# Last expert's rows of the others, constants issued from ScalarE, and output halves stored before the overflow loop

## What is computed

```python
for i in range(DEPTH):                       # DEPTH = 2
    h = rms_norm(x, ln_mix[i])
    y = dilated_attention(h, ...) if i == 0 else rwkv7_bidirectional(h, ...)
    x = x + y
    h = rms_norm(x, ln_ffn[i])
    x = x + (swiglu(h, f_w13, f_w2) if i == 0 else moe_swiglu(h, router, w13, w2))

def moe_swiglu(h, router, w13, w2):          # 8 experts, the best 2 of each token
    top_val, top_idx = lax.top_k((t @ router), 2)
    gate = jax.nn.softmax(top_val, axis=-1)
    for e in range(8):
        out = out + combine[:, e:e + 1] * swiglu(t, w13[e], w2[e])
```

## Time and profile before

| | |
|---|---|
| time, median of 3 runs | 1946.71 us (1943.17 to 1948.93) |
| time of the profiled execution | 1941.92 us |
| its span | 1940.0 us |
| PE busy | 1851.5 us (95%) |
| DVE, ACT, POOL busy | 761.2, 286.0, 198.0 us |
| read from HBM | 460.04 MB |

### The profile page before, as it was taken

How to read it: one execution, slowest core, us unless ns; L and a number is a source line. 1 busy time by engine, 2 the same in 40 slices (tenths; PEclk the granted TensorE clock), 3 DMA queues, 4 the chain that set the end, 5 groups by cost and what they waited for, 6 DMA issues and landing times.

```text
span 1940.0 us, 35245 instructions
## 1 busy us (share of the span) xinstructions
PE 1851.5 (95%) x15348; PEld 1123.1 (58%) x15348; DVE 761.2 (39%) x2119; ACT 286.0 (15%) x611; POOL 198.0 (10%) x318
## 2 busy tenths in 40 slices
PE   7998998999998999889879999999999999999997
PEld 3445445677763558788745555555555555555453
DVE  3114113100007255866335535344353534445333
ACT  2113113000000225434210000000000000000000
POOL 1110110100001233642200000000000000000000
PEclk9999999999998999999989999999999999999998
DMA  9442351635542101100267999999999999999992
GB/s 362 170 137 80 132 172 44 195 131 173 148 173 87 38 9 23 29 21 7 93 261 281 414 404 407 406 392 417 399 415 402 405 409 395 415 404 406 416 371 99
DMA packets 137631, 472.49 MB, mean 244 GB/s; under 512 B 30104, under 2 KB 59056, under 8 KB 94464
## 3 DMA queue, kind: packets, MB, share of 16 engines
q1 hardware_dynamic: 134592, 460.05, 61.6%
q0 software_dynamic: 2080, 7.37, 1.2%
q10 hardware_dynamic: 800, 2.76, 0.4%
HBM read 460.04 MB, written 10.10 MB: 242 GB/s over the span
## 4 chain that ended last, share of the span: by engine, by line
PE 87%; DVE 6%; ACT 2%; DMA 2%; issue 1%; SPq 0%; POOL 0%; DVEq 0%; POOLq 0%
PE ps L1275 19%; PE ps L679 13%; PE ps L801 13%; PE ps L1251 10%; PE ps L1283 10%; PE ps L739 8%; PE ps L1258 5%; PE ps L752 3%; PE ps L855 2%; PE ps L768 1%; DMA arena<-yd,arena 1%; PE ps L1199 1%; DVE arena L1883 1%; PE ps L687 1%; PE ps L1206 1%
## 5 line engine op out<-in xcount | busy, mean ns | idle before, releaser
L1275 PE MATMUL ps<-arena 128*64 128x256 f32 x3584 | 397.1, 379 | 0.7 <-DVE arena L2096 0.7
L679 PE MATMUL ps<-arena 128*128 128x128 f32 (+11 forms) x2114 | 334.2, 332 | 33.4 <-DVE arena L1870 9.1
L1275 PEld LDWEIGHTS ps<-arena 128*64 128x64 f32 x3584 | 255.9, 137 | 151.2 <-issue 29.0
L679 PEld LDWEIGHTS ps<-arena 128*128 128x128 f32 (+4 forms) x2114 | 248.2, 187 | 111.1 <-issue 56.5
L801 PE MATMUL ps<-arena 128*128 128x512 f32 x576 | 251.6, 592 | 2.0 <-DMA arena<-wqkv 2.0
L2146 DVE TENSOR_TENSOR arena<-arena,ps 64x256 f32<-64x256 f32 x168 | 71.3, 426 | 395.4 <-ACT arena L1583 395.2
L1283 PE MATMUL ps<-arena 128*32 128x256 f32 x3584 | 205.7, 381 | 0.5 <-issue 0.5
L1251 PE MATMUL ps<-arena 128*64 128x512 f32 x896 | 203.3, 598 | 0.0
L801 PEld LDWEIGHTS ps<-arena 128*128 128x128 f32 x576 | 107.4, 190 | 127.7 <-issue 125.3
L1583 ACT ACTIVATE arena<-ps 64x256 f32<-64x256 f32 x168 | 63.2, 376 | 751.2 <-PE ps L1275 550.3
L1283 PEld LDWEIGHTS ps<-arena 128*32 128x32 f32 x3584 | 111.6, 110 | 89.1 <-issue 22.4
(11 more groups left out here) (249 smaller groups left out, 1222.5 us busy)
## 6 DMA issues: line engine op xcount, KB each, us to landing
arena<-mw SPq DMA_DIRECT2D x336, 1024.0 KB, 11.8
arena<-wqkv SPq DMA_DIRECT2D x36, 1024.0 KB, 8.6
arena<-fw SPq DMA_DIRECT2D x32, 1024.0 KB, 6.7
arena<-wrkv SPq DMA_DIRECT2D x12, 1024.0 KB, 6.4
arena<-awo SPq DMA_DIRECT2D x4, 1024.0 KB, 6.2
arena<-bwo SPq DMA_DIRECT2D x4, 1024.0 KB, 9.9
xg<-arena POOLq DMA_DIRECT2D x8, 384.0 KB, 9.4
arena<-xg SPq DMA_DIRECT2D x7, 384.0 KB, 15.7
```

Of the source, the lines that this page charges most:

```text
L679: last = mm(o, a, b, start=(n == 0), stop=(n == len(pairs) - 1))
L1275: last = mm(ps[r, g % 4, 0:256], picked[:, b, k, 0:64], w[:, k, a * 256:(a + 1) * 256], start=(k == 0), stop=(k == KB - 1))
```

## The change

It has four parts.

1. The five small loads leave SP's queue and are issued by ACT, as its first instructions, `vec` ahead of `const`. SP goes from x straight to `wqkv`.
2. In the last expert, `add_rows` is no longer called once after j = 2 (the first pair). `add_rows(0)` adds the first row of each token after j = 8, and `add_rows(1)` the second after j = 11.
3. `scatter` writes its four products to four PSUM banks (4, 7, 0, 1), and PE's waits on `back_sb` are gone.
4. SP stores each half of x as soon as `add_back` is done with it, and only then reads `many` and goes through its overflow loop. Stores inside that loop would repeat the output if a body were entered. `experts_done` is gone, and at the end SP waits for both stores.

```diff
--- before.py
+++ after.py
@@ -498,11 +497,6 @@
 
             for t in range(T):
                 sp.dma_start(x[:, t, :], x_in[t * P:(t + 1) * P, :]).then_inc(in_x[t], 16)
-            sp.dma_start(const[:, 0:C_TRI], const_in[:, 0:C_TRI]).then_inc(in_const, 16)
-            sp.dma_start(vec, vec_in).then_inc(in_vec, 16)
-            sp.dma_start(pos_i, pos_in).then_inc(in_small, 16)
-            sp.dma_start(qkc, qk_cols).then_inc(in_small, 16)
-            sp.dma_start(qkr, qk_rows.partition_broadcast(P)).then_inc(in_small, 16)
             for u in range(U_QKV):
                 if u == 6:
                     sp.dma_start(const[:, C_TRI:C_ALL], const_in[:, C_TRI:C_ALL]).then_inc(in_mask, 16)
@@ -651,12 +645,16 @@
                 expert_unit(item, EXPERTS // 2 - 1)
                 next_rows(item, EXPERTS // 2 - 1)
 
+            for t in range(T):
+                sp.wait_ge(back_sb, 2 * t + 2)
+                sp.dma_start(out[t * P:(t + 1) * P, :], x[:, t, :]).then_inc(out_done, 16)
             sp.wait_ge(over_ok, 1)
             many = sp.value_load(over_i[0:1, 0:1], min_val=0, max_val=OVER)
             with sp.Fori(0, OVER) as j:
                 with sp.If(j < many):
                     e = sp.value_load(over_i[0:1, bass.ds(j + (OVER + 1), 1)], min_val=0, max_val=EXPERTS - 1)
                     sp.wait_ge(down_ps, j * (GE // 2) + EXPERTS * GE // 2)
+                    sp.wait_ge(out_done, j * 32 + 32)
                     freed = [(up_ps, 3 * (n // 2) + 3) if kind == "up" else (down_ps, n + 1) for kind, n, _ in over_plan]
                     for kind, n, u in over_plan:
                         if u >= R:
@@ -664,9 +662,10 @@
                             per = UPS if s is up_ps else GE // 2
                             sp.wait_ge(s, j * per + (EXPERTS * per + c))
                         tiled_unit(u, (mw13 if kind == "up" else mw2)[bass.ds(e, 1), n])
-            sp.wait_ge(experts_done, 1)
-            sp.dma_start(out.rearrange("(t p) n -> p t n", p=P), x).then_inc(out_done, 16)
-            sp.wait_ge(out_done, 16)
+                    for t in range(T):
+                        sp.wait_ge(back_sb, j * 4 + (2 * t + 6))
+                        sp.dma_start(out[t * P:(t + 1) * P, :], x[:, t, :]).then_inc(out_done, 16)
+            sp.wait_ge(out_done, 32)
 
 
         @block.tensor
@@ -1239,9 +1238,7 @@
                 pe.wait_ge(pickT_sb, back)
                 for k in range(4):
                     t, h = k // 2, k % 2
-                    if k >= 2:
-                        pe.wait_ge(back_sb, back * 4 + (k - 5))
-                    run(ps[:, (4, 7)[k % 2], :], [(pickT[0:width, b, t, :], yb[0:width, h * 512:(h + 1) * 512])]).then_inc(back_ps, 1)
+                    run(ps[:, (4, 7, 0, 1)[k], :], [(pickT[0:width, b, t, :], yb[0:width, h * 512:(h + 1) * 512])]).then_inc(back_ps, 1)
 
             def expert(n, c, b, plan, landed, before_last=None):
 
@@ -1330,6 +1327,12 @@
 
         @block.scalar
         def _(act):
+            act.dma_start(vec, vec_in).then_inc(in_vec, 16)
+            act.dma_start(const[:, 0:C_TRI], const_in[:, 0:C_TRI]).then_inc(in_const, 16)
+            act.dma_start(pos_i, pos_in).then_inc(in_small, 16)
+            act.dma_start(qkc, qk_cols).then_inc(in_small, 16)
+            act.dma_start(qkr, qk_rows.partition_broadcast(P)).then_inc(in_small, 16)
+
             steps = Steps(act, act_step)
 
             def rms_squares(n, junk, added=None):
@@ -2115,7 +2118,7 @@
                     t, h = n // 2, n % 2
                     cols = slice(h * 512, (h + 1) * 512)
                     dve.wait_ge(back_ps, c * 4 + (n - 3))
-                    dve.scalar_tensor_tensor(x[:, t, cols], ps[:, (4, 7)[n % 2], :], weight(t), x[:, t, cols], ALU.mult, ALU.add).then_inc(back_sb, 1)
+                    dve.scalar_tensor_tensor(x[:, t, cols], ps[:, (4, 7, 0, 1)[n], :], weight(t), x[:, t, cols], ALU.mult, ALU.add).then_inc(back_sb, 1)
 
             def first_turned(pair):
 
@@ -2137,7 +2140,7 @@
                         last = dve.transpose(o[:, a, :, 64:CAP], src[:, :, j, :])
                 return last
 
-            def expert(n, stored, at_second=None, next_b=None):
+            def expert(n, stored, add_rows=None, next_b=None):
 
                 for j in range(UPS):
                     p = j // 3
@@ -2152,8 +2155,8 @@
                     if j % 3 == 2:
                         dve.wait_ge(hide_sb, n * UPS + (j + 1))
                         last_turned(p).then_inc(hidT_sb, 1)
-                    if j == 2 and at_second:
-                        at_second()
+                    if j in (8, 11) and add_rows is not None:
+                        add_rows((j - 8) // 3)
                     if j in (11, 14) and next_b is not None:
                         next_picked(n, next_b, (j - 11) // 3)
                 dve.wait_ge(down_ps, n * (GE // 2) + GE // 2)
@@ -2196,13 +2199,15 @@
                     link(dve.tensor_reduce(share[:, k], missing[:, :, 0:n], AX, ALU.add))
                 link(dve.tensor_tensor(share[:, 1], share[:, 1], twice[:, 0], ALU.mult))
 
-            def add_rows():
-
-                for k in range(2):
-                    dve.wait_ge(ya_in, 64)
-                    for t in range(T):
-                        dve.scalar_tensor_tensor(x[:, t, :], ya[:, k, t, :], share[:, k, t:t + 1], x[:, t, :], ALU.mult, ALU.add).then_inc(added, 1)
-                    dve.wait_ge(added, 2 * k + 2)
+            def add_rows(k):
+
+                dve.wait_ge(ya_in, 64)
+                if k:
+                    dve.wait_ge(added, 2 * k)
+                for t in range(T):
+                    dve.scalar_tensor_tensor(x[:, t, :], ya[:, k, t, :], share[:, k, t:t + 1], x[:, t, :], ALU.mult, ALU.add).then_inc(added, 1)
+                if k:
+                    dve.wait_ge(added, 4)
 
             choose(0, lambda t: place[:, t, 0:1])
             picked_out(1, 0, CAP)
@@ -2230,7 +2235,8 @@
                     picked_out(j + 2, 0, CAP)
                     expert(j + EXPERTS, EXPERTS * 16)
                     add_back(j + 2, lambda t: comb[:, t, bass.ds(e + 1, 1)])
-            dve.memset(over_f, 0.0).then_inc(experts_done, 1)
+                    dve.wait_ge(out_done, j * 32 + 64)
+                    dve.memset(over_f, 0.0)
 
 
         @block.gpsimd
```

More of the change, by code:

```diff
@@ L365, in build @@
             sem(n) for n in ("up_ps", "sge_sb", "hide_sb", "rows_turned", "hidT_sb", "down_ps", "result_sb", "back_ps", "back_sb"))
-        experts_done = sem("experts_done")
         in_lora, d_ready, mix_ready, mix_ps, mix_sb, ones_ok = (sem(n) for n in ("in_lora", "d_ready", "mix_ready", "mix_ps", "mix_sb", "ones_ok"))
```

## The result

The changed kernel takes 1927.11 us (median of 6 runs, 1926.88 to 1929.73), the kernel before 1945.5 us (6 runs, 1943.17 to 1948.93). The ratio is 0.9915, 95% interval 0.9904 to 0.9927, so 16.5 us less (14.2 to 18.7). The plain difference of the two medians is 18.4. The direction was right. The profiled execution took 1926.94 us against 1941.92, its span is 1925.0 against 1940.0: 15.0 us less.

What follows compares the result with a forecast made beforehand. It took PE to bound the kernel (87% of the last chain), so changes pay where PE idles, runs slowly or has finished. Terms 1.3 + 7.9 + 0 + 2.8 = 12.0 us, off the 1946.71 median: 1934.7 us, range 1929 to 1940.

Steps and rivals of the forecast that it cites:

- Part 1, 1.3 us: At the start, issuing the small loads on ACT lets the first `wqkv` unit land earlier, 1.3 us less.
- the 0.4 to 0.7: At the start, the low end of the gain, if a second issuer saves only issuing time: 0.4 to 0.7 us.
- `hT` is not what limits PE next: At the start, with weights landing at 12.3, PE's matmul 7 starts at 15.4, after `hT`'s last block at 14.26.
- Part 2, 7.9 us: In the last expert, moving the additions removes PE's wait and the low clock behind it: 7.9 us, between 7.3 and 8.0.
- where I had said 8: In the last expert, DVE reaches the moved additions 8 us after the gathered rows land, so it need not wait.
- The feared shortage of weights: In the last expert, PE waits once for weights (or products), 1942.7 us, chance 0.07; or outruns them for good, 1953, 0.04.
- Part 3 and the scatter: At the end, four banks remove a wait that had cover: 0 us gained, at most 0.3.
- ±1.7: In the scatter, the spell of low clock may fall differently: a spread of 1.7 us either way.
- Part 4, 2.8 us: At the end, stores first: span ends at 1937.2 against 1940.0 with SP's first pass at 3.6; 1.7 to 3.5 less.
- DVE's own loop ends at 1935.4 and hides behind SP's: At the end, DVE's overflow loop finishes at 1935.4, before SP's, which ends the span at 1937.2.
- an empty loop would now be on the path: At the end, SP's overflow loop, unseen before, becomes the last thing in the span, some 8 us long.
- 15.1 as its high end: Over the whole kernel, the terms' high ends sum to 13.4 us, with 1.7 more by the clock.

Runs made afterwards that it cites:

- a1: The kernel before with only the two pairs of additions moved behind the third and fourth pair of the last expert; 1933.8 us.
- a3: The kernel before with only the stores put ahead of the overflow loops, scatter still on two banks; 1940.75 us.
- f1: The kernel before with eight more PE transposes into an unread bank between the last down product and the scatter; 1942.26 us.
- b1: The changed kernel with the load of `qk_rows` issued by SP behind unit 0 of `wqkv`, the other four small loads still on ACT; 1928.24 us.
- e1: The changed kernel with the additions one pair earlier, behind the second and third pair of the last expert; 1930.25 us.
- a4: The changed kernel with the four additions back behind the first pair of the last expert; 1938.15 us.
- b3: The changed kernel with the scatter on two banks and PE's waits on the additions back; 1930.33 us.
- b2: The changed kernel with one test of `many` > 0 around the whole overflow loop on SP, PE, ACT and DVE; 1926.65 us.
- d0: The changed kernel measured once more, unaltered, beside three variants of its end; 1929.11 us.
- a2: The kernel before with only the five small loads issued by ACT; 1941.5 us.

## Why the prediction was wrong in size, point by point

Measured was 7.6 us below the forecast of 1934.7. 4.6 of it are the base, a step that I did not see as one: I took terms read from one profile off the median of three runs, 1946.71, which lay 4.8 above the profiled execution of before, while the changed kernel's median lies 0.2 above its profiled execution. The other 3.0 are terms: the scatter, put at 0, was 1.7; 1.5 lie where nothing was changed and I had no term; part 4 was 0.5 too small, and part 1 0.8 too large.

**Part 1, 1.3 us: too large.** The two traces give 0.54. Over the profiles, the first product starts at 13.95 with the loads on SP (before, a1, a3, f1) and at 13.0 with all five on ACT (eight kernels), 0.95 less. The step that failed is "a rate of 219 at a share of 0.80 is mostly waiting inside packets, which is what a second queue can cover". The second queue covered nothing: b1 shows that the low rate belongs to one load, `qk_rows`, which the change let run against unit 0 just as before. The Trainium skill's rule (DMA: Bandwidth & Descriptors, "Issuing engines are not separate DMA queues") stood nearer to the first pair of traces, with the 0.4 to 0.7 that I had worked out for it (0.4 should be 0.5: 2 × 0.25 / 1.05); the 0.95 lies between 0.7 and my 1.3. That `hT` is not what limits PE next was right.

**Part 2, 7.9 us: right.** It was 7.96 in the two traces, both the stall and the low clock behind it, and the additions cost nothing in their new place. DVE began the first two at 1839.58, 40.0 us behind expert 6's end at 1799.58. In e1, whose gather is waited for, the rows landed 32.8 behind it (1837.03 less 1804.24), so the margin is some 7 us, where I had said 8. The feared shortage of weights did not come.

**Part 3 and the scatter: the banks right, the base wrong.** The four banks give 0 at low clock, as argued (6.19 with two in before and a3, 6.19 with four in a4 and e1), and 0.25 at high clock (b3). The step that failed is the 0 for the scatter with "±1.7" around it. The trace of before was at low clock there, so the only way it could differ was up. It did, by 1.69, of which 1.45 are the clock.

Whether that was luck is open. Of the twelve profiles in which PE idled 1.85 us before the scatter, all four with the stall had low clock in it, and of the eight without it only e1. In a1 the additions alone were moved, and the clock stayed high. So the 1.45 may well belong to part 2, as a consequence that I had not foreseen. In all five the clock was still high when the scatter began and fell 0.9 to 1.7 us later. The stretches of the scatter of before, with the columns of the earlier trace rows:

```profile
1922.87:1923.72 0.85, 0.85 (x2) 0.49 (x3) 0.00 (x0) 0.00 (x0) 0.00 (x0) 1.00 0.00 0
1923.72:1927.13 3.41, 3.41 (x5) 1.24 (x4) 1.50 (x2) 0.00 (x0) 0.00 (x0) 0.50 0.00 0
```

**Part 4, 2.8 us: a little small.** It was 3.27. SP's first pass took 2.4 us and not 3.6, which would have given 4.0 us. "DVE's own loop ends at 1935.4 and hides behind SP's" was wrong: DVE's first pass took 3.5 and not the 2.9 of the earlier trace rows, and its loop came last. That an empty loop would now be on the path was right, and b2 prices it: with one test in place of five passes the span ends 2.5 us earlier, and then the store is what ends last. a3 shows how little a size of the first pass can be relied on. There SP's took 0.6 us:

```profile
L658 SPq COMPARE_BRANCH  x5: 40/45/54, 1933.4 to 1936.1; - x5
L659 SPq COMPARE_BRANCH  x5: 50/50/60, 1932.8 to 1935.7; - x5
```

In the traces of before, changed and a3, each first pass of over 2 us has a packet of the profile's instruction queues inside it (in the changed kernel at 1919.7 in SP's and at 1918.5 in DVE's). Those of a3's SP and of ACT (0.3 us) have none.

**What had no term.** 1.54 us lie where nothing was changed: 1.12 in expert 0, where PE slowed and stood still in the trace of before, with nothing that the profile shows to wait for, and not in that of the changed kernel, and 0.42 in the middle. The line in the profile of before, in its timeline, is this:

```profile
1033.64 1.94 PE L1283 MATMUL ps<-arena 128*32 128x256 f32 x28 [0.49 <-issue]
```

Expert 0 is as long in eight more profiles, the changed kernel's second one (d0) among them, and not in the other five. So it isn't the change. What it is stays open: the four kernels a1 to a4, which ran together, all lack it, and the eight that ran later all have it. The middle alone varied from 1008.26 to 1013.14 over the 14 profiles.

**The range.** These two and the scatter's clock make a difference of two single traces uncertain by several us, and I had given that part 1.7. The median of three runs, 1946.71, was also high: later medians of before are 1945.5, 1943.7, 1944.3 and 1943.91. From 1943.9 the same terms and the same width would have given 1931.9, in a range of 1926.2 to 1937.2, which holds the 1927.11. My own sum had 15.1 as its high end, and 3.5 more for the runs; the low bound of 1929 did not even take these in fully (1946.71 − 15.1 − 3.5 = 1928.1). Beside the repeated measure of 15.2 us (d0), the forecast of 12.0 was short by the missing 1.7 of the scatter and the parts above.

What stays open: why a2's times gained 3.1 us where its trace has 0.6, and what decides in a given execution whether the clock falls in the scatter. On the first, the table has a hint and no more: expert 0 begins at 1025.4 us on average with the loads on SP (1023.7 to 1026.3, four profiles) and at 1023.8 with all five on ACT (1022.7 to 1026.4, eight profiles).

## What to carry to other kernels

An operation that waits for a late transfer costs by what is queued behind it, not by how long it waits: behind pair 0 a wait of 18 us cost 8 us, behind pair 1 a wait of 8.6 cost nothing (e1). An empty runtime loop has a price as soon as it stands behind the last result; test once around it, and it is one jump. Terms read from a profile are to be taken off the profiled execution's time, and the distance from there to the median of the runs is a term of its own. And before a forecast rests on two single traces, look for terms in the first that are chance, such as a low clock or a gap with nothing shown to wait for, and give each its own place in the range, on the side to which it can go.

## What the runs showed of the hardware

- While a load of 96 KB that reads one row of 768 bytes 128 times was under way, all 16 DMA engines together moved 219, 235 and 249 GB/s over 2 us (before from 6 to 8, changed from 8 to 10, b1 from 11 to 13), against 391 to 406 behind it. It was so from either queue and in each of these three places.
- The first pass of an empty loop, from its jump over the body to the loop's next compare, took 3.8 to 4.9 us on SP while the weights' transfers ran (before, a1, a2, f1), 2.4 to 2.7 with that traffic over and 0.6 in a3. It took 2.9 to 4.1 on DVE, 3.6 to 4.1 on PE, and 0.3 on ACT. Each later pass took 0.7 to 0.8 on SP, DVE and PE.
- PE's clock fell to 1.2 GHz in the scatter, after PE had idled 1.85 us before it, in five of twelve profiles. Against high clock with the same number of banks it cost 1.45 us (before, a3), 1.7 (a4, e1) and 1.8 (a2).
- The clock's spells in the middle differ between executions. Up to 1020 us the clock was low for 44.4 us in e1 (middle 1013.14) and for 37.5 in b1 (1008.26). At half speed that is some 3.5 of the 4.9 us between them; the rest is open. From 910 to 960 us, e1 and then b1:

```profile
910.00:960.00 50.00, 42.79 (x632) 38.95 (x627) 22.49 (x48) 12.03 (x23) 15.64 (x23) 0.93 0.27 91
```

```profile
910.00:960.00 50.00, 45.03 (x674) 40.44 (x672) 21.81 (x42) 13.23 (x25) 15.65 (x23) 0.97 0.28 91
```
